# Group norm sums and factors in the free banks of the z panels, next group's transposes spread over the last two panels

## The chip, the cores and the metric

The kernel runs on one core of a Trainium2 chip (trn2). Its time is the device time of one execution in microseconds (us). Engines are named as in the profile: PE is the matrix engine (PEld its weight loads), DVE the vector engine, ACT the scalar engine, POOL the GpSimd engine, SP the engine that issues most loads.

## What is computed

The reference is a two-layer backbone over 512 latent and 256 context tokens of width 1024. Layer 0 mixes tokens with HGRN2, layer 1 with a bidirectional Mamba-2 scan; each ends with a SwiGLU network. The change lies in the Mamba-2 mixer:

```python
def prep(h):
    z, xbc, dt = jnp.split(h @ w_in, [SSM_D_INNER, SSM_D_INNER + SSM_CONV_DIM], axis=-1)
    xbc = jax.nn.silu(centred_depthwise_conv(xbc, conv_w, conv_b))
    xs, bm, cm = jnp.split(xbc, ...)
    ...
def readout(y_f, y_b, xs, z):
    y = (y_f + y_b + d_skip[:, None] * xs).reshape(bsz, m, SSM_D_INNER) * jax.nn.silu(z)
    y = rmsnorm(y.reshape(bsz, m, SSM_GROUPS, SSM_D_INNER // SSM_GROUPS),
                norm_w.reshape(SSM_GROUPS, -1)).reshape(bsz, m, SSM_D_INNER)
    return y @ w_out
```

There are 4 groups of 512 channels (8 heads of 64). A group's y is normalized over its own 512 channels: a sum of squares for each token, a factor 1/sqrt(mean + eps), and a product with both the factor and a weight.

## The kernel before, in words

Every float32 product is made of three float32r ones: an operand is split into a high part (`whi`, `hhi`, by ACT) and a low part (`wlo`, `hlo`, by DVE), and `product_block` (L309) issues high*high, high*low, low*high for one of the 8 slices k of the inner dimension. A **panel** is one 128-column slice of the weights: SP loads it to `raw`, ACT splits it at L292 (`whi`), DVE at L296 (`wlo`), PE multiplies it in 8 blocks of k. The weights of panel n+2 are split once panel n is finished. Panels take the two slots of the PSUM tensor G in turn; a slot has two banks of 512 columns. `Gq[:, b]` is bank b of G (0 and 1 are slot 0, 2 and 3 slot 1). The other four banks of PSUM are the tensor S; `PAIR[0]` is its banks 0 and 1, `PAIR[1]` its banks 2 and 3.

`ss_all` runs the mixer as a loop over groups in which **two groups overlap**. One call handles the ten panels j = 0 to 9 of group g (four x, b, c, four z) and, between their blocks, the scan and the norm of group q = g - 1. The first call has no q, three calls in a loop on the engines have both, the last has no g (there the blocks of the next product, `so_beside`, stand between). Panels 0 to 4 (x and b) cover all 768 tokens and need both banks of their slot; c and z (j = 5 to 9) cover 512 and use the first bank alone. Within a call (j, k) is a place on PE, after block k of panel j:

- j = 0 to 2: the chunk chain of q, 12 steps at every second k (`chain_tensor`, L1487 and L1491). Step n needs a weighted copy `wx` of `xtm`, made by DVE in `chain_values` (L1444). `chain_vector` makes `wx` of step n + 1, and at n = 0 also that of step 0.
- j = 3 to 6: the heads of q. (7, 3): transposes of their result `ytm` into S (L1605). DVE adds it to `yb` (semaphore `ya`), multiplies by z (`yz`), ACT squares (`ysq`), DVE adds the squares into `wx0` (L1568, `yr`).
- (8, 1): the sums over channels (L1610), to bank 0 of S. DVE makes the mean (L615), POOL the power (L620), and at (8, 4) PE spreads the factors over the partitions (L609), to bank 1 of S. DVE scales the four tiles of `yb` (L1578, `yn`), ACT makes their high parts (`ybhi`, L1424, `yh`), DVE their low parts (`yblo`, L1582, `yl`), and POOL stores both in memory (`y_park`, L1810).
- j = 9: six **turns** for the next chain, of group g: transposes of b into PAIR[0] (turn 0, L1625), the products of b and c into bank 2 of S (turn 1, L1628), four tiles of x (turns 2 to 5, L1633) into PAIR[0] and PAIR[1] in turn. ACT copies each out (`btm`, `cb`, `xtm`; L1428, L1431, L1434). Turn 0 waits until `yn` says that the factors in bank 1 have been read.

POOL's writes to `y_park` must have landed (`yout`) before ACT overwrites `yb` at j = 1 (L1409) and DVE writes `ytm` at chain step 4. All engines run their own queue in program order and wait for each other on semaphores only.

Of the kernel before, what the change touches and what calls it, by code (L numbers as in the profile page):

```python
# [199 lines left out]
def program(nc, x, c, ctx_x, c_ctx, ada_w, ada_b, norm_w, ffn_w_in, ffn_w_out, final_norm_w, hg_w_in, hg_lb,  # L200
            hg_norm_w, hg_w_out, ssm_w_in, ssm_conv_w, ssm_conv_b, ssm_dt_bias, ssm_a_log, ssm_d, ssm_norm_w,
            ssm_w_out, out):
    with ExitStack() as ctx:
# [1145 lines left out]
        def ss_scalar(act, dt, ss, g, q, prev):  # L1349
# [21 lines left out]
            for j in range(len(PANELS)):  # L1371
# [49 lines left out]
                if q is not None and j == 8:  # L1421
# [4 lines left out]
                if ss is not None and j == 9:  # L1426
                    act.wait_ge(s["ytr"], 6 * g + 1)
                    act.activation(m["btm"][:, :, :].rearrange("p b n -> p (b n)"), PAIR[0][:, 0:T], ACT.Copy)\  # L1428
                        .then_inc(s["stc"], 1)
                    act.wait_ge(s["ytr"], 6 * g + 2)  # L1430
                    act.activation(m["cb"][:, :], S[:, 2, :], ACT.Copy).then_inc(s["stc"], 1)  # L1431
                    for i_ in range(GT):
                        act.wait_ge(s["ytr"], 6 * g + 3 + i_)
                        act.activation(m["xtm"][:, :, i_ * P:(i_ + 1) * P],  # L1434
                                       PAIR[i_ % 2][:, 0:T].rearrange("p (b n) -> p b n", n=P), ACT.Copy)\
                            .then_inc(s["stc"], 1)
# [10 lines left out]
        def chain_vector(dve, q, n):  # L1447
            d, k, b = chain_at(n)
            st, own = m[f"st{d}"], states_of[d]
            if n == 0:  # L1450
                chain_values(dve, q, 0)
# [56 lines left out]
        def ss_vector(dve, dt, ss, g, q, prev):  # L1508
            for j in range(len(PANELS)):
# [60 lines left out]
                if q is not None and j == 8:  # L1570
                    dve.wait_ge(s["ysum"], q + 1)
                    mean_dve(dve, S[:, 0, 0:LBLK], GW)
# [3 lines left out]
                    for i_ in range(GT):  # L1576
                        yb = m["yb"][:, i_, :]
                        dve.scalar_tensor_tensor(yb, yb, m["colA"][:, bass.ds(q * GT + (COL_SN + i_), 1)],  # L1578
                                                 S[:, 1, :], ALU.mult, ALU.mult).then_inc(s["yn"], 1)
# [6 lines left out]
        TURNS = {0: 0, 1: 1, 2: 2, 3: 3, 5: 4, 7: 5}  # L1586

        def ss_between(pe, g, q, j, k):

            if q is not None:  # L1590
# [16 lines left out]
                if (j, k) == (8, 1):  # L1607
                    pe.wait_ge(s["yr"], GT * q + GT)
                    for b in range(LBLK):
                        ins = pe.matmul(S[:, 0, b:b + 1], block(m["wx0"][:, :], b), ones[:, :],  # L1610
                                        start=True, stop=True)
                    ins.then_inc(s["ysum"], 1)
                if (j, k) == (8, 4):
                    spread_pe(pe, q + RSTD_GROUPS, range(LBLK), S[:, 1, :])
            elif (j, k) == DT_TURN:
                dt_turn(pe)
            if g is not None and j == 9 and k in TURNS:
                n = TURNS[k]
# [522 lines left out]
```

## Time and profile before

| what | value |
|---|---|
| median of 3 runs | 2251.61 us (2251.16 to 2253.8) |
| profiled execution, its time | 2257.25 us |
| its span (first to last instruction) | 2254.3 us |
| PE busy | 2126.8 us, 94% of the span |
| DVE busy | 1091.2 us, 48% |
| ACT busy | 825.8 us, 37% |
| POOL busy | 50.4 us, 2% |
| granted PE clock, mean | 0.97 of full speed |

The median is 5.6 us below the profiled execution and 2.7 us below its span. The mixer's group loop lies at about 1338 to 1805 us of the span. A row of the timeline has the start, the length, engine, line, operation and, in brackets, how long the engine stood idle before it and on what. Matmuls overlap, so lengths on PE are longer than the distance from one start to the next. A float32 matmul is two instructions, so 4 of them are x8. In the "windows" rows PEclk is the granted clock as a share of 2.4 GHz: 1.00 is that level, 0.50 is 1.2 GHz, and values between are a mixture.

### The profile page before, as it was taken

How to read it: one execution, taken by the hardware profiler on the slowest of the kernel's cores; microseconds unless marked ns; L12 is line 12 of the kernel's file. 1: busy time of each engine (PE TensorE's matmuls, PEld its weight loads, DVE VectorE, ACT ScalarE, POOL GpSimd, SP SyncE). 2: the span in 40 equal slices, each digit the busy share in tenths (PEclk: the TensorE clock that was granted, in tenths of full speed). 3: DMA queues.
4: the chain of work that ended last, by engine and by line, in shares of the span. 5: the costliest groups of instructions: out<-in, count | busy, mean ns of one | idle time of the engine just before them, and what ended most of it. 6: DMA issues, size and time to landing. Idle time of an engine off the chain costs nothing.

```text
span 2254.3 us, 33844 instructions
## 1 busy us (share of the span) xinstructions
PE 2126.8 (94%) x13412; PEld 1892.8 (84%) x13412; DVE 1091.2 (48%) x1607; ACT 825.8 (37%) x1278; POOL 50.4 (2%) x79
## 2 busy tenths in 40 slices
PE   5899999999989999999999889999998898999998
PEld 3899999998889999999999867777775687888887
DVE  4755555557452222222234757767676545333334
ACT  2543334334232221122222454737382425532322
POOL 1000000000000000000000100000000000000000
PEclk8999999999989999999999989999999899999999
DMA  7322222213323332233321221221215232332332
GB/s 270 125 76 85 76 85 85 82 60 113 112 75 112 114 98 76 85 112 112 97 77 47 79 57 37 66 64 43 79 47 177 75 94 69 99 109 84 97 102 75
DMA packets 297512, 204.42 MB, mean 91 GB/s; under 512 B 5012, under 2 KB 289037, under 8 KB 295629
## 3 DMA queue, kind: packets, MB, share of 16 engines
q1 hardware_dynamic: 293965, 180.03, 26.4%
q0 software_dynamic: 3456, 23.09, 2.8%
q8 instruction: 68, 1.11, 0.2%
q14 instruction: 23, 0.19, 0.0%
HBM read 189.47 MB, written 13.63 MB: 90 GB/s over the span
## 4 chain that ended last, share of the span: by engine, by line
PE 78%; DVE 11%; ACT 7%; issue 3%; DMA 1%; SPq 0%; ACTq 0%; DVEq 0%; POOL 0%
PE G L309 65%; PE G L415 2%; PE S L1491 1%; ACT whi L292 1%; PE S L765 1%; DVE acc L1522 1%; ACT e L1367 1%; DVE hlo L646 1%; PE S L736 1%; PE S L1487 1%; DVE hn L638 1%; DVE wlo L296 1%; DVE cum L985 1%; PE S L1671 1%; PE G L421 1%
## 5 line engine op out<-in xcount | busy, mean ns | idle before, releaser
L309 PE MATMUL G<-hhi,whi 128*128 128x384 f32 (+2 forms) x2336 | 731.8, 371 | 31.2 <-DVE hlo L646 20.1
L309 PE MATMUL G<-hlo,whi 128*128 128x384 f32 (+2 forms) x2336 | 683.8, 351 | 0.0
L309 PE MATMUL G<-hhi,wlo 128*128 128x384 f32 (+2 forms) x2336 | 683.8, 351 | 0.0
L296 DVE TENSOR_TENSOR wlo<-raw,whi 128x1024 fp32r<-128x1024 f32 (+1 forms) x225 | 288.1, 1281 | 810.4 <-ACT whi L292 810.1
L292 ACT ACTIVATE whi<-raw 128x1024 fp32r<-128x1024 f32 (+1 forms) x225 | 248.7, 1106 | 958.0 <-PE G L309 487.5
L309 PEld LDWEIGHTS G<-hhi,whi 128*128 128x128 f32 x2336 | 425.2, 192 | 99.3 <-issue 36.3
L309 PEld LDWEIGHTS G<-hhi,wlo 128*128 128x128 f32 x2336 | 435.0, 191 | 20.7
L309 PEld LDWEIGHTS G<-hlo,whi 128*128 128x128 f32 x2336 | 435.8, 192 | 18.1
L309 PE MATMUL G<-mhi,whi 128*128 128x384 f32 (+2 forms) x550 | 165.6, 346 | 0.0
L309 PE MATMUL G<-mlo,whi 128*128 128x384 f32 (+2 forms) x550 | 165.2, 345 | 0.0
L309 PE MATMUL G<-mhi,wlo 128*128 128x384 f32 (+2 forms) x550 | 165.2, 345 | 0.0
L1522 DVE SCALAR_TENSOR_TENSOR acc<-xpad,colC,acc 128x770 f32<-128x770 f32 (+1 forms) x96 | 93.6, 975 | 35.2 <-ACT acc L1399 27.9
L309 PEld LDWEIGHTS G<-mhi,whi 128*128 128x128 f32 x550 | 101.2, 188 | 6.1
L309 PEld LDWEIGHTS G<-mlo,whi 128*128 128x128 f32 x550 | 101.3, 188 | 6.0
L309 PEld LDWEIGHTS G<-mhi,wlo 128*128 128x128 f32 x550 | 101.2, 188 | 6.0
L620 POOL TENSOR_TENSOR rstd<-stat,mhalf 128x6 f32<-128x6 f32 (+3 forms) x22 | 27.1, 1232 | 2097.7 <-DVE stat L615 2097.7
L1367 ACT ACTIVATE e<-S,shiftT 128x128 f32<-128x128 f32 x256 | 69.8, 394 | 9.2 <-PE S L1660 8.9
L1084 ACT ACTIVATE mhi<-mid 128x768 f32 (+3 forms) x44 | 32.5, 740 | 95.7 <-DVE mid L1104 95.7
L1135 DVE SCALAR_TENSOR_TENSOR x<-G,mods,x 128x384 f32 (+7 forms) x99 | 49.1, 533 | 20.0 <-PE G L309 18.5
L1491 PE MATMUL S<-wx,btm 128*128 128x512 f32 x80 | 45.0, 650 | 14.3 <-DVE wx L1444 14.3
L919 DVE SCALAR_TENSOR_TENSOR sin<-sin,gl,S 128x128 f32<-128x128 f32 x160 | 54.9, 348 | 6.7 <-PE S L736 1.6
L1108 DVE TENSOR_TENSOR mlo<-mid,mhi 128x768 f32 (+3 forms) x44 | 36.3, 825 | 44.2 <-ACT mhi L1084 44.2
(277 smaller groups left out, 2098.4 us busy)
## 6 DMA issues: line engine op xcount, KB each, us to landing
raw<-in_ffn_w_in_dram SPq DMA_DIRECT2D x88, 512.0 KB, 3.7
raw<-in_ffn_w_out_dram SPq DMA_DIRECT2D x32, 704.0 KB, 4.5
raw<-in_ssm_w_in_dram SPq DMA_DIRECT2D x41, 512.0 KB, 3.8
raw<-in_hg_w_in_dram SPq DMA_DIRECT2D x40, 512.0 KB, 3.9
adaw<-in_ada_w_dram SPq DMA_DIRECT2D x20, 1024.0 KB, 6.1
adaf<-in_ada_w_dram SPq DMA_DIRECT2D x20, 1024.0 KB, 5.0
ada<-in_ada_w_dram SPq DMA_DIRECT2D x4, 2048.0 KB, 13.2
raw<-in_ssm_w_out_dram SPq DMA_DIRECT2D x16, 512.0 KB, 3.9
```

Of the source, the lines that this page charges most:

```text
L292: act.activation(whi[pn.slot][:, 0:kt, :], raw[pn.slot][:, 0:kt, :], ACT.Copy).then_inc(s["hi"], 1)
L296: dve.tensor_tensor(wlo[pn.slot][:, 0:kt, :], raw[pn.slot][:, 0:kt, :], f32(whi[pn.slot][:, 0:kt, :]), ALU.subtract).then_inc(s["lo"], 1)
L309: ins = pe.matmul(G[:, tl.slot, g0:g0 + n], w[pn.slot][:, k, :], r[:, k_base + k, t0:t0 + n], start=(first and k == 0 and i == 0), stop=(l ...
L415: ins = pe.matmul(to[o:o + 2, :], m["csil"][:, k, :], w[:, k, :], start=(k < STRIPS), stop=(k >= KT - STRIPS))
L620: pool.tensor_tensor(m["rstd"][:, b0:b1], m["stat"][:, b0:b1], m["mhalf"][:, b0:b1], ALU.pow)\
L919: dve.scalar_tensor_tensor(to, sin[d][:, cc, :], gl[d][:, cc:cc + 1], new, ALU.mult, ALU.add).then_inc(own, 1)
L1084: act.activation(m["mhi"][:, bass.ds(i, 1), 0:nt].rearrange("p a t -> p (a t)"), m["mid0"][:, 0:nt], ACT.Copy).then_inc(s["mhi"], 1)
L1108: dve.tensor_tensor(m["mlo"][:, bass.ds(i, 1), 0:nt].rearrange("p a t -> p (a t)"), m["mid0"][:, 0:nt], f32(m["mhi"][:, bass.ds(i, 1), 0:n ...
L1135: ins = dve.scalar_tensor_tensor(xj, G[:, tl.slot, g0:g0 + n], gate, xj, ALU.mult, ALU.add)
L1367: ins = act.activation(block(m[f"e{d}{r}"][:, :], b), block(S[:, d, :], b), ACT.Exp, bias=m["shiftT"][:, b, bass.ds(q * HPG + (d * NH + hh ...
L1491: pe.matmul(S[:, d, :], m["btm"][:, b, :], m[f"wx{d}"][:, :], start=True, stop=True).then_inc(s["ds"], 1)
L1522: dve.scalar_tensor_tensor(m["acc"][:, 0:n], xpad[ci % 2][:, k:k + n], m["colC"][:, bass.ds(conv_tile(kind, i, g) + k * CONV_TILES, 1)], m ...
```

## The change

In a call with both groups the sums go to bank 1 of G and the factors to bank 3, the second banks of the slots, which z panels leave free. They stand at (8, 3) and (8, 6). The six turns stand at (8, 1), (8, 2), (8, 5), (8, 7), (9, 1), (9, 3). Turn 0 waits for `ya` (DVE has read the S banks) in place of `yn`; a new wait for `yn` stands at (9, 7), ahead of the next x panel, which needs bank 3. ACT copies turns 0 to 2 out at its step j = 8, turns 3 to 5 at j = 9, and only then makes `ybhi`. DVE makes the first `wx` of the next chain at j = 9 and the low parts `yblo` behind it; in the call before they stood at j = 8, ahead of the split of a panel. The first call keeps its six turns at their places, but its DVE too makes the first `wx` at j = 9. The last call keeps banks and places.

```diff
@@ ss_scalar (ACT)
-                if q is not None and j == 8:
+                if ss is not None:
+                    for n in ((0, 1, 2) if j == 8 else (3, 4, 5) if j == 9 else ()) if q is not None else range(6 * (j == 9)):
+                        turn_out(act, g, n)
+                if q is not None and j == (8 if ss is None else 9):
                     for i_ in range(GT):
                         act.wait_ge(s["yn"], q * GT + (i_ + 1))
                         act.activation(m["y3hi" if ss is None else "ybhi"][:, i_, :], m["yb"][:, i_, :], ACT.Copy)\
                             .then_inc(s["yh"], 1)
-                if ss is not None and j == 9:
-                    act.wait_ge(s["ytr"], 6 * g + 1)
-                    act.activation(m["btm"][:, :, :].rearrange("p b n -> p (b n)"), PAIR[0][:, 0:T], ACT.Copy)\
-                        .then_inc(s["stc"], 1)
...
+        def turn_out(act, g, n):
+            act.wait_ge(s["ytr"], 6 * g + n + 1)
+            if n == 0:
+                ins = act.activation(m["btm"][:, :, :].rearrange("p b n -> p (b n)"), PAIR[0][:, 0:T], ACT.Copy)
+            elif n == 1:
+                ins = act.activation(m["cb"][:, :], S[:, 2, :], ACT.Copy)
+            else:
+                ins = act.activation(m["xtm"][:, :, (n - 2) * P:(n - 1) * P],
+                                     PAIR[n % 2][:, 0:T].rearrange("p (b n) -> p b n", n=P), ACT.Copy)
+            ins.then_inc(s["stc"], 1)
@@ chain_vector (DVE)
-            if n == 0:
-                chain_values(dve, q, 0)
@@ ss_vector (DVE)
                 if q is not None and j == 8:
                     dve.wait_ge(s["ysum"], q + 1)
-                    mean_dve(dve, S[:, 0, 0:LBLK], GW)
+                    mean_dve(dve, group_sums(ss)[:, 0:LBLK], GW)
...
-                                                 S[:, 1, :], ALU.mult, ALU.mult).then_inc(s["yn"], 1)
+                                                 group_factors(ss), ALU.mult, ALU.mult).then_inc(s["yn"], 1)
+                if ss is not None and j == 9:
+                    chain_values(dve, g, 0)
+                if q is not None and j == (8 if ss is None else 9):
                     for i_ in range(GT):
                         dve.wait_ge(s["yh"], q * GT + (i_ + 1))
...
-        TURNS = {0: 0, 1: 1, 2: 2, 3: 3, 5: 4, 7: 5}
-
-        def ss_between(pe, g, q, j, k):
+        def group_sums(ss):
+            return S[:, 0, :] if ss is None else Gq[:, 1, :]
+        def group_factors(ss):
+            return S[:, 1, :] if ss is None else Gq[:, 3, :]
+        TURNS_FIRST = {(9, 0): 0, (9, 1): 1, (9, 2): 2, (9, 3): 3, (9, 5): 4, (9, 7): 5}
+        TURNS = {(8, 1): 0, (8, 2): 1, (8, 5): 2, (8, 7): 3, (9, 1): 4, (9, 3): 5}
+        SUMS_BESIDE, SPREAD_BESIDE = (8, 3), (8, 6)
+        def ss_between(pe, ss, g, q, j, k):
...
-                if (j, k) == (8, 1):
+                if (j, k) == ((8, 1) if ss is None else SUMS_BESIDE):
...
-                if (j, k) == (8, 4):
-                    spread_pe(pe, q + RSTD_GROUPS, range(LBLK), S[:, 1, :])
+                if (j, k) == ((8, 4) if ss is None else SPREAD_BESIDE):
+                    spread_pe(pe, q + RSTD_GROUPS, range(LBLK), group_factors(ss))
+                if ss is not None and (j, k) == (9, KT - 1):
+                    pe.wait_ge(s["yn"], q * GT + GT)
...
-            if g is not None and j == 9 and k in TURNS:
-                n = TURNS[k]
+            turns = TURNS_FIRST if q is None else TURNS
+            if g is not None and (j, k) in turns:
+                n = turns[j, k]
                 if n == 0:
                     pe.wait_ge(s["conv"], 6 * g + 6)
-                    pe.wait_ge(s["dtT"], 1)
-                    if q is not None:
-                        pe.wait_ge(s["yn"], q * GT + GT)
+                    if q is None:
+                        pe.wait_ge(s["dtT"], 1)
+                    else:
+                        pe.wait_ge(s["ya"], q * GT + GT)
```

On PE, panel 8 of the loop, before: the sums (L1610, waiting for `yr`) are the first thing between the blocks.

```order
L309 MATMUL G<-hlo,whi_71 128x512
L309 MATMUL G<-hhi,wlo_72 128x512
L1608 ISA
L1610 MATMUL S<-ones,wx_168 128x1 [waits s_yr]
L1610 MATMUL S<-ones,wx_168 128x1 x3
L309 MATMUL G<-hhi,whi_71 128x512
L309 MATMUL G<-hlo,whi_71 128x512
L309 MATMUL G<-hhi,wlo_72 128x512
```

The same place after; L1642 and L1645 are turns 0 and 1, L1623 the sums.

```order
L1640 ISA [waits s_conv]
L1642 MATMUL S<-ident,bfm 128x128 [waits s_ya]
L1642 MATMUL S<-ident,bfm 128x128 x5
L309 MATMUL G<-hhi,whi_71 128x512
L309 MATMUL G<-hlo,whi_71 128x512
L309 MATMUL G<-hhi,wlo_72 128x512
L1645 MATMUL S<-cfm,bfm 128x128 x4
L309 MATMUL G<-hhi,whi_71 128x512
L309 MATMUL G<-hlo,whi_71 128x512
L309 MATMUL G<-hhi,wlo_72 128x512
L1623 MATMUL G<-ones,wx_168 128x1 [waits s_yr]
L1623 MATMUL G<-ones,wx_168 128x1 x3
```

Two turns and two blocks have moved ahead of the sums. On DVE, from the end of a call over the loop's edge, before:

```order
L1582 TENSOR_TENSOR yblo<-yb,ybhi 128x512 [waits s_yh] x4
L295 REGISTER_ALU
L296 TENSOR_TENSOR wlo_72<-raw_68,whi_71 128x1024 [waits s_hi]
L1677 REGISTER_ALU
L1677 COMPARE_AND_BRANCH
L296 TENSOR_TENSOR wlo_70<-raw_67,whi_69 128x1024 [waits s_hi]
L1533 CAST sel<-ident 64x8 x4
L1444 TENSOR_TENSOR wx_168<-xtm,wT 128x512 [waits s_stc]
L1444 TENSOR_TENSOR wx_169<-xtm,wT 128x512
L1477 COPY st_170<-S 128x512 [waits s_ds]
```

And after:

```order
L296 TENSOR_TENSOR wlo_72<-raw_68,whi_71 128x1024 [waits s_hi]
L1447 ISA [waits s_stc]
L1447 TENSOR_TENSOR wx_168<-xtm,wT 128x512
L1586 TENSOR_TENSOR yblo<-yb,ybhi 128x512 [waits s_yh] x4
L1694 REGISTER_ALU
L1694 COMPARE_AND_BRANCH
L296 TENSOR_TENSOR wlo_70<-raw_67,whi_69 128x1024 [waits s_hi]
L1534 CAST sel<-ident 64x8 x4
L1447 TENSOR_TENSOR wx_169<-xtm,wT 128x512
L1478 COPY st_170<-S 128x512 [waits s_ds]
```

The first `wx` has moved ahead of the edge; `wx1`, of step 1, stays behind the split and the four casts. On ACT, steps j = 8 and 9, before:

```order
L292 ACTIVATE whi_69<-raw_67 128x1024 [waits s_pan]
L1381 ISA
L1381 ACTIVATE z<-G 128x512
L1424 ACTIVATE ybhi<-yb 128x512 [waits s_yn] x4
L291 REGISTER_ALU [waits s_raw1]
L292 ACTIVATE whi_71<-raw_68 128x1024 [waits s_pan]
L1381 ISA
L1381 ACTIVATE z<-G 128x512
L1428 ACTIVATE btm<-S 128x768 [waits s_ytr]
L1431 ACTIVATE cb<-S 128x512 [waits s_ytr]
L1434 ACTIVATE xtm<-S 128x6x128 [waits s_ytr] x3
```

And after:

```order
L1433 ACTIVATE btm<-S 128x768 [waits s_ytr]
L1435 ACTIVATE cb<-S 128x512 [waits s_ytr]
L1437 ACTIVATE xtm<-S 128x6x128 [waits s_ytr]
L291 REGISTER_ALU [waits s_raw1]
L292 ACTIVATE whi_71<-raw_68 128x1024 [waits s_pan]
L1381 ISA
L1381 ACTIVATE z<-G 128x512
L1437 ACTIVATE xtm<-S 128x6x128 [waits s_ytr] x2
L1431 REGISTER_ALU
L1437 ACTIVATE xtm<-S 128x6x128 [waits s_ytr]
L1427 ACTIVATE ybhi<-yb 128x512 [waits s_yn] x4
```

The high parts of y have moved behind all copies, to the end of the call.

## Rows read from the trace of the kernel before

**Rows 1.** The page: the chain that ended last, by engine.

```profile
PE 78%; DVE 11%; ACT 7%; issue 3%; DMA 1%; SPq 0%; ACTq 0%; DVEq 0%; POOL 0%
```

**Rows 2.** Waits of PE, 1330:1830: who waited for whom, total, times, longest.

```profile
PE S L1491 <- DVE wx L1444: 14.3, 5, 4.2
PE S L1610 <- DVE wx L1568: 11.1, 4, 4.2
```

**Rows 3.** Timeline of PE, first loop call, panel 7 to the next panel 0.

```profile
1441.17 1.10 PE L1671 MATMUL S<-xtm,e 128*128 128x64 f32 x8 [1.42 <-DVE e L1500]
...
1449.18 0.39 PE L309 MATMUL G<-hhi,wlo 128*128 128x512 f32 x1
1451.98 1.05 PE L1610 MATMUL S<-ones,wx 128*128 128x1 f32 x8 [2.42 <-DVE wx L1568]
...
1458.23 0.40 PE L309 MATMUL G<-hhi,whi 128*128 128x512 f32 x1
...
1458.92 0.39 PE L309 MATMUL G<-hhi,whi 128*128 128x512 f32 x1
...
1460.71 0.84 PE L1625 MATMUL S<-ident,bfm 128*128 128x128 f32 x6 [0.27 <-DVE yb L1578]
...
1469.70 0.59 PE L309 MATMUL G<-hhi,whi 128*128 128x384 f32 x2
...
1474.17 2.00 PE L1491 MATMUL S<-wx,btm 128*128 128x512 f32 x2 [3.17 <-DVE wx L1444]
...
1478.86 1.02 PE L1491 MATMUL S<-wx,btm 128*128 128x512 f32 x2
...
1481.80 1.02 PE L1491 MATMUL S<-wx,btm 128*128 128x512 f32 x2
```

**Rows 4.** Timeline of PE at the other three joints, in order of time.

```profile
1347.68 0.59 PE L309 MATMUL G<-hhi,whi 128*128 128x384 f32 x2
...
1352.16 2.08 PE L1491 MATMUL S<-wx,btm 128*128 128x512 f32 x2 [3.17 <-DVE wx L1444]
...
1357.87 1.20 PE L1491 MATMUL S<-wx,btm 128*128 128x512 f32 x2
...
1574.33 1.05 PE L1610 MATMUL S<-ones,wx 128*128 128x1 f32 x8 [2.39 <-DVE wx L1568]
...
1591.89 0.59 PE L309 MATMUL G<-hhi,whi 128*128 128x384 f32 x2
...
1600.99 1.02 PE L1491 MATMUL S<-wx,btm 128*128 128x512 f32 x2
...
1696.21 1.87 PE L1610 MATMUL S<-ones,wx 128*128 128x1 f32 x8 [2.09 <-DVE wx L1568]
...
1714.93 0.82 PE L1633 MATMUL S<-ident,xfm 128*128 128x128 f32 x6
1719.98 4.62 PE L1491 MATMUL S<-wx,btm 128*128 128x512 f32 x6 [4.23 <-DVE wx L1444]
```

**Rows 5.** Timeline of DVE, first loop call: norm, and start of the chain.

```profile
1457.84 2.72 DVE L1578 SCALAR_TENSOR_TENSOR yb<-yb,colA,S 128x512 f32<-128x512 f32 x4 [4.61 <-PE S L609]
...
1471.77 1.23 DVE L296 TENSOR_TENSOR wlo<-raw,whi 128x1024 fp32r<-128x1024 f32 x1 [7.66 <-ACT whi L292]
...
1473.43 1.29 DVE L1444 TENSOR_TENSOR wx<-xtm,wT 128x512 f32<-128x512 f32 x2
```

**Rows 6.** Timeline of ACT, same call.

```profile
1458.63 2.61 ACT L1424 ACTIVATE ybhi<-yb 128x512 fp32r<-128x512 f32 x4 [6.27 <-DVE yb L1578]
...
1469.98 0.81 ACT L1434 ACTIVATE xtm<-S 128x768 f32<-128x768 f32 x1 [1.24 <-PE S L1633]
1470.69 1.05 ACT L292 ACTIVATE whi<-raw 128x1024 fp32r<-128x1024 f32 x1
```

**Rows 7.** Windows, PE alone: stretch, length, PE busy (instructions), PEclk, DMA share, GB/s.

```profile
1352.00:1358.00 6.00, 5.84 (x15) 0.50 0.33 89
...
1453.50:1457.50 4.00, 4.00 (x17) 0.57 0.46 131
```

**Rows 8.** DMA issues: size each, median us from issue to landing.

```profile
y_park_lo<-yblo POOLq DMA_DIRECT2D x3, 1024.0 KB, 6.4
```

More of the change, by code:

```diff
@@ L1425, in ss_scalar @@
                             .then_inc(s["yh"], 1)
-                if ss is not None and j == 9:
-                    act.wait_ge(s["ytr"], 6 * g + 1)
-                    act.activation(m["btm"][:, :, :].rearrange("p b n -> p (b n)"), PAIR[0][:, 0:T], ACT.Copy)\
-                        .then_inc(s["stc"], 1)
[L1430 to L1436, printed above, removed]
+        def turn_out(act, g, n):
[8 more added lines that the diff above has]
+            ins.then_inc(s["stc"], 1)
         def chain_values(dve, q, n):
@@ L1606, in ss_between @@
                         ins.then_inc(s["ytt"], 1)
-                if (j, k) == (8, 1):
+                if (j, k) == ((8, 1) if ss is None else SUMS_BESIDE):
                     pe.wait_ge(s["yr"], GT * q + GT)
                     for b in range(LBLK):
-                        ins = pe.matmul(S[:, 0, b:b + 1], block(m["wx0"][:, :], b), ones[:, :],
+                        ins = pe.matmul(group_sums(ss)[:, b:b + 1], block(m["wx0"][:, :], b), ones[:, :],
                                         start=True, stop=True)
                     ins.then_inc(s["ysum"], 1)
-                if (j, k) == (8, 4):
-                    spread_pe(pe, q + RSTD_GROUPS, range(LBLK), S[:, 1, :])
+                if (j, k) == ((8, 4) if ss is None else SPREAD_BESIDE):
+                    spread_pe(pe, q + RSTD_GROUPS, range(LBLK), group_factors(ss))
+                if ss is not None and (j, k) == (9, KT - 1):
+                    pe.wait_ge(s["yn"], q * GT + GT)
             elif (j, k) == DT_TURN:
                 dt_turn(pe)
-            if g is not None and j == 9 and k in TURNS:
-                n = TURNS[k]
+            turns = TURNS_FIRST if q is None else TURNS
+            if g is not None and (j, k) in turns:
+                n = turns[j, k]
                 if n == 0:
                     pe.wait_ge(s["conv"], 6 * g + 6)
-                    pe.wait_ge(s["dtT"], 1)
-                    if q is not None:
-                        pe.wait_ge(s["yn"], q * GT + GT)
+                    if q is None:
+                        pe.wait_ge(s["dtT"], 1)
+                    else:
+                        pe.wait_ge(s["ya"], q * GT + GT)
                     for b in range(NBLK):
@@ L1641, in ss_tensor @@
                     product(pe, ss + j, ss + j, m["hhi"], m["hlo"], KT, LAT if kind in "zc" else SEGS,
-                            between=lambda k: ss_between(pe, g, q, j, k))
+                            between=lambda k: ss_between(pe, ss, g, q, j, k))
                 else:
                     for k in range(KT):
-                        ss_between(pe, None, q, j, k)
+                        ss_between(pe, None, None, q, j, k)
                         for _ in range(SO_BESIDE.get((j, k), 0)):
```

## The prediction

> **What bounds the kernel now.** I read the chain that ended last first: 78% of it is PE [rows 1]. So what counts is where PE stands still, and the view for that is the list of waits. In the mixer's loop two waits lead it: the first chain step waits 14.3 us in 5 places for `wx`, and the sums wait 11.1 us in 4 places for the squares [rows 2]. One of the four, in the last call, isn't touched by the change. The timeline then shows what stands around each wait. In panel 8 PE reaches (8, 1) at about 1449.4, finds `wx0` not summed and starts the sums at 1451.98 [rows 3]. Behind it come two blocks, the factors, and in panel 9 all six turns. At the next panel 0 PE does one block and stands for 3.17 us. The timelines of ACT and DVE say why: the last copy of x starts at 1469.98, `whi` follows it at once, `wlo` starts at 1471.77, then come four casts, and the first `wx` starts at 1473.43 [rows 5, 6]. This `wx` has had its data since 1470.8; it stands late only because it is behind a split in DVE's program.
>
> The windows show the second price. After the sums' wait the granted clock is 0.57 of full over 1453.5 to 1457.5, and after the first joint's wait it is 0.50 for 6 us [rows 7]; 0.50 is the 1.2 GHz level. After the 1.42 us wait at 1441.17 [rows 3] the blocks run on at full pace. So each long wait costs itself and a slow stretch, and I take both from distances between starts.
>
> **Part 1: from (8, 1) to the next panel 0.** The work is the same before and after: 14 blocks, six turns, sums, factors. Its length without waits at the full clock: from turn 0 at 1460.71 to panel 0 at 1469.70 are 7 blocks and six turns, 9.0 us. The other 7 blocks take 0.69 each (1458.23 to 1458.92, three matmuls), 4.8. Sums 1.05 by their row; the factors are 8 matmuls too, I take 1.05 again. Sum 15.9 us [rows 3]. Before, the stretch begins where PE went idle (start of the sums less the idle time less 0.15 for the end of the last matmul) and takes 1449.4 to 1469.7 = 20.3; 1571.8 to 1591.9 = 20.1; 1694.0 to 1715.5 = 21.5 (the last turn at 1714.93 plus 0.6) [rows 3, 4]. If all waits go, the gain is 4.4 + 4.2 + 5.6 = **14.2 us**. Of it 7.3 are the waits themselves, the rest is slow clock and 0.3 to 0.4 before turn 0.
>
> Do they go? Sums: PE now does turn 0 (0.6), turn 1 (0.8) and two blocks (1.5) before them and comes at 1452.3, with the squares' sum ready at 1451.9. Margin 0.4 us; if I am off by that, the cost is as much for each call. Turn 0 needs `ya`, which DVE has done some 3 us before. Factors: three blocks and turn 2 lie between them and the sums, 2.8 us; before it was three blocks. They come at 1456.1 and DVE scales from about 1457.3 to 1460.3 (2.72 for four, rows 5), while the new wait at (9, 7) is reached at 1465.3. Cover 5 us, cost nothing; the wait holds back only panel 0. Turns: each needs the copy of the turn two before it. ACT's copies take 0.8 each; the tightest is turn 5 at 1462.3, behind the copy of turn 3, which on ACT stands behind `whi` and z of panel 8 and ends about 1460.6. Cost nothing, cover 1.7 us. DVE's split of a panel at j = 9 is needed only at 1465.3 and comes no later.
>
> **Part 2: the joint, panel 0 to the second chain step.** Without a wait: one block 1.15 (1469.70 to where the idle 3.17 begins), then step 0 and two blocks, 2.94 (1478.86 to 1481.80), together 4.1 us [rows 3]. Before it took 10.2, 9.2 and 9.1 us (1347.68 to 1357.87; 1469.70 to 1478.86; 1591.89 to 1600.99) [rows 3, 4]. After, counted from panel 0's start E: in the first call the turns stay, the copy of the last ends at E + 1.1 and `wx` of 0.65 at E + 1.8, while PE is there at E + 1.15. A wait of 0.7 us stays. In the loop the last turn is at (9, 3), 3.4 us before E, its copy ends at E - 1.8 and `wx0` is ready at E - 1.1. That wait goes whole. Next is `wx1`: ACT makes the four `ybhi` (2.6, rows 6) from E - 1.9 to E + 0.7, `whi` to E + 1.75, DVE `wlo` to E + 3.0, casts 0.5, `wx1` to **E + 4.1**; PE wants it at E + 4.1. So it just meets, and I charge 0.1. Gains 5.4 + 5.0 + 4.9 = **15.3 us**, if the slow stretch goes with the wait; a remaining 0.7 is well below the 1.42 that left no trace.
>
> **Part 3: the last call's start** has no panel beside it. PE waits 4.23 us, then DVE is the busier [rows 4]. After, DVE has one `wx` less in the row (0.65) and needn't wait for step 0's matmul (about 1.5). Bounds 0.65 and the whole 4.4; I take **2.2**, the sum of the two.
>
> **Part 4: what moves later.** `yblo` ends at E + 1.5 where it ended 7 us before E, so the store of it is issued at about E + 1.8. It lands 6.4 us later [rows 8], E + 8.2. ACT's next write of `yb` and DVE's chain step 4 wait for it; that step comes at E + 13 in the loop and E + 11 in the last call. Cover 3 to 5 us, cost nothing. In the last call POOL's reloads of y go out 2 us later and behind two stores of 1 MB; the first product that reads them comes 17 us after E. Cost nothing to 2 us. Sum: 14.2 + 15.3 + 2.2 = 31.7; I take off 0.7 for hand-overs that came out as just meeting. **31 us**: the execution of span 2254.3 would have 2223, and the median 2251.6 becomes **2220.6**.
>
> **Rivals.** (a) The wait moves one chain step on: `wx1` comes at the lag it has now, E + 5.0, so 0.95 us for each loop joint, and with that the slow stretches at the joints stay (2.8 + 1.7 + 1.7). For it: the margin is zero, and ACT has 2.6 us of `ybhi` ahead of `whi`. Against it: a wait of 1.42 us left the clock alone. 8 us of the gain go: 2229. (b) The slow stretch behind the sums isn't due to the wait. Its half level begins 1.7 us after PE has resumed, not in the wait, and PE was full before and after. Then 6.5 us of part 1 stay: 2227. The Trainium skill ("TensorE: Matmul & The Clock Gate", section on HAM oscillation) ties the slow clock to idle gaps above a length; if 2.4 us is too short, its rule gives this rival, and the trace, with a slow stretch behind all three such waits, speaks rather against it. (c) The change gains nothing: the waits go, but panels 0 to 2 are held by the taps and the chain on DVE. PE's back-to-back steps of 2.94 speak against it. 2251. (d) **Slower**: the stores of y hold the next group. Place: DVE's chain step 4 at (1, 0), with PE's steps behind it; price: each us that a store lands after E + 11 to 13, in three calls, at once on the path. It decides from a landing time of 9 to 11 us in place of 6.4 and passes the 31 us gained only from about 20 us each; nothing in the rows comes near. 2260.
>
> **How the numbers follow.** Forecast 0.68, (a) 0.12, (b) 0.10, (c) 0.03, (d) 0.02, more gain than summed (last call's 4.4 whole, further slow stretches gone) 0.05. The range goes from 2214 (34.6 by the upper bounds, and 3 us of clock) to 2234 ((a) and (b) in good part together). Faster by over 0.2% (4.5 us, about what a measurement of this kernel can tell): 0.95; within 0.2%: 0.03; slower: 0.02.
>
> **What would show it.** In the profile after, the waits of PE should have no row of the sums in the three loop calls, the one for `wx` should be one of about 0.7 us in the first call and the last call's; windows over panels 8, 9 and 0 should show PEclk 1.00; panel 8's (8, 1) to panel 0 should take 16 us, panel 0 to step 1 4.1 to 4.5. The clock is the weakest step: if half-level stretches stand where no wait is, I am wrong by up to 13 us. Next comes `wx1`.

## The result, and the profile after

| | before | after |
|---|---|---|
| median, us (range, executions) | 2251.97 (2251.16 to 2253.8, 4) | 2224.68 (2224.3 to 2229.35, 4) |
| profiled execution, us | 2257.25 | 2224.3 |
| its span, us | 2254.3 | 2222.4 |
| its mean granted clock | 0.970 | 0.977 |

The changed kernel takes 0.9882 of the time before (95% interval 0.9866 to 0.9898): 27 us less by the medians, with 30 to 23 us inside the interval. The forecast was 31 us less, at 2220.6, in a range of 2214 to 2234. It held. A second comparison of the same two kernels (below) gave 0.9856 (0.9841 to 0.9871), 32 us less by the ratio and 31 by the medians.

The first thing to see is PE's list of waits over the same stretch as [rows 2], 1330 to 1830 (waiting engine and line, who was waited for, total us, times, longest):

```profile
PE S L1675 <- ACT e L1367: 7.0, 7, 2.4
...
PE S L1623 <- DVE wx L1569: 4.2, 1, 4.2
PE S L1492 <- DVE wx L1447: 3.5, 2, 2.9
```

The sums (L1610 before, L1623 now) waited 11.1 us in four places and now wait 4.2 in one, the last call's, which the change leaves alone. The first chain step (L1491 before, L1492 now) waited 14.3 us in five places and now 3.5 in two: 0.58 in the first call and 2.90 in the last. That is 17.7 us of waiting gone. The waits on `e`, inside the heads, lead the list now (7.0 us, 6.9 before).

PE's timeline of the first loop call, to be laid beside [rows 3] (start, us, engine, line, operation, out<-in, count, idle time before it):

```profile
1444.69 0.82 PE L1642 MATMUL S<-ident,bfm 128*128 128x128 f32 x6
...
1447.64 0.95 PE L1623 MATMUL G<-ones,wx 128*128 128x1 f32 x8
...
1460.36 0.51 PE L309 MATMUL G<-hhi,whi 128*128 128x384 f32 x2
...
1461.42 1.02 PE L1492 MATMUL S<-wx,btm 128*128 128x512 f32 x2
...
1464.40 1.02 PE L1492 MATMUL S<-wx,btm 128*128 128x512 f32 x2
```

Turn 0, turn 1 and two blocks stand where PE used to wait, the sums follow without idle time, and the next panel 0 starts 15.67 us after turn 0. Its second chain step comes 4.04 us after panel 0. Both have been at full pace all the way, as windows of PE alone say (stretch, length, PE busy and instructions, PEclk, DMA share, GB/s); [rows 7] had 0.50 and 0.57 at these places, that is at or near the lower of TensorE's two levels, 1.2 in place of 2.4 GHz:

```profile
1346.40:1351.40 5.00, 4.42 (x24) 1.00 0.04 7
1444.00:1460.00 16.00, 16.00 (x99) 1.00 0.25 66
1460.00:1465.00 5.00, 5.00 (x26) 1.00 0.62 226
```

So the gain can be split in two. Over 1330 to 1800, the time at the lower level fell from 54.5 us to 27.3 (each window's length times twice what its clock lacks to 1.00). PE is nearly always busy there, so this gives back about half of it, 13.6 us. With the 17.7 us of waits that makes 31.3, beside 31.9 measured between the two spans. (Outside this stretch the time at the lower level hardly changed, 81.1 us before and 79.1 after.)

The start of the last call, which [rows 4] show at 1719.98 with a wait of 4.23 us, and the first call's joint:

```profile
1348.31 1.13 PE L1492 MATMUL S<-wx,btm 128*128 128x512 f32 x2 [0.58 <-DVE wx L1447]
...
1351.36 1.02 PE L1492 MATMUL S<-wx,btm 128*128 128x512 f32 x2
...
1688.28 4.64 PE L1492 MATMUL S<-wx,btm 128*128 128x512 f32 x6 [2.90 <-DVE wx L1447]
```

### The profile page after: what moved, and what is told of

Its sections match the earlier page's. It is cut to its first block, busy times and chain, and to the rows that moved or that the text cites. A ratio compares the mean times of both kernels' runs of the same rounds, so it can differ in the third digit from the quotient of the medians.

```text
span 2222.4 us, 33823 instructions
## 1 busy us (share of the span) xinstructions
PE 2111.2 (95%) x13397; PEld 1882.9 (85%) x13412; DVE 1091.4 (49%) x1607; ACT 824.9 (37%) x1278; POOL 49.1 (2%) x79
## 4 chain that ended last, share of the span: by engine, by line
PE 79%; DVE 10%; ACT 6%; issue 3%; DMA 1%; SPq 0%; ACTq 0%; DVEq 0%; POOL 0%
PE G L309 66%; PE G L415 2%; PE S L765 1%; PE S L1492 1%; DVE acc L1523 1%; ACT whi L292 1%; ACT e L1367 1%; DVE hlo L646 1%; PE S L736 1%; PE S L1488 1%; DVE wlo L296 1%; DVE hn L638 1%; PE S L1688 1%; DVE cum L985 1%; PE G L421 1%
## 5 line engine op out<-in xcount | busy, mean ns | idle before, releaser
L309 PE MATMUL G<-hhi,whi 128*128 128x384 f32 (+2 forms) x2336 | 726.8, 369 | 31.7 <-DVE hlo L646 20.5
L1523 DVE SCALAR_TENSOR_TENSOR acc<-xpad,colC,acc 128x770 f32<-128x770 f32 (+1 forms) x96 | 93.7, 976 | 36.2 <-ACT acc L1399 28.3
L573 ACT ACTIVATE hhi<-hn,mods 128x128 fp32r<-128x128 f32 (+2 forms) x64 | 30.2, 503 | 51.6 <-DVE hn L638 51.6
```

Of the source, the lines that this page charges most:

```text
L309: ins = pe.matmul(G[:, tl.slot, g0:g0 + n], w[pn.slot][:, k, :], r[:, k_base + k, t0:t0 + n], start=(first and k == 0 and i == 0), stop=(l ...
L573: ins = act.activation(m["hhi"][:, v % KT, t0:t0 + n], hn_of(N, v)[:, t0:t0 + n], ACT.Identity, bias=mod(l, 3 * i, v % KT, g))
L1523: dve.scalar_tensor_tensor(m["acc"][:, 0:n], xpad[ci % 2][:, k:k + n], m["colC"][:, bass.ds(conv_tile(kind, i, g) + k * CONV_TILES, 1)], m ...
```

## Experiments

Each ratio is to the kernel before, run on the same chip beside it, with its 95% interval. "Slow stretch" is short for one in which the windows show PEclk near 0.50. The kernel before was measured three times more beside them, at 2252.95, 2253.15 and 2252.3 us in the median.

### The change again

The same kernel a second time, as the measure for those beside it.

> The changed kernel itself, once more, beside its variants. Expected: 2224.7 us as measured, ratio to before 0.988. If the 1.24 us that it was ahead before the first changed instruction was chance, the ratio stays where the median had it and not where the profiled spans had it (0.986).

Measured: 2221.76 us (2219.72 to 2225.39, 4 executions), 0.9856 (0.9841 to 0.9871). The two intervals for the same change, around 0.9882 and 0.9856, only just meet. The ratio came out where the two profiled spans had it (0.986). The lead of 1.2 us ahead of the first changed instruction didn't recur: panel 0 of the second call starts at 1347.59 here, at 1346.44 in the first profile and at 1347.68 before. From this panel 0 to the first block that multiplies the last group's own y (`y3hi`, in the last call) the two profiles of the changed kernel take 423.9 and 423.8 us. This stretch is called the changed part from here on; the kernel before takes 455.4 us for it (1347.68 to 1803.09).

### Each half of the change alone

`sums_only` keeps the free banks and the early turns, but puts the first `wx` back where it stood:

```diff
         def chain_vector(dve, q, n):
+            if n == 0:
+                chain_values(dve, q, 0)
...
-                if ss is not None and j == 9:
-                    chain_values(dve, g, 0)
```

> After, but the first wx is made as before, at the start of the next call behind the split and the casts. Part 1 alone. My theory: the stretch from (8, 1) to panel 0 takes 15.7 us as in after (gain 14.2 to 14.9 in all), the joints wait about 3.0 us for wx0 and have the half clock behind it (8.8 us in the loop, 10.2 in the first call): 2252 - 15 = 2237. Rival (b), slow stretches that aren't due to the wait: 2243.

`wx_only` is the kernel before with nothing but the first `wx` moved ahead of the next panel's split on DVE:

```diff
-            if n == 0:
-                chain_values(dve, q, 0)
...
                         dve.tensor_tensor(m["yblo"][:, i_, :], m["yb"][:, i_, :],
...
+                if ss is not None and j == 9:
+                    chain_values(dve, g, 0)
```

> Before, and DVE makes the first wx at j = 9. Part 2 alone. My theory: the last turn stays at (9, 7), so wx0 comes 1.8 us after panel 0's start, where PE is at 1.15: 0.7 us of wait stays at each joint and the clock stays full. Gains 5.4 + 4.4 + 4.3, and 2 in the last call: 2236. The waits for the sums stay at 2.2 to 2.6 us with their slow stretches. Rival: the slow stretch at the joint stays though the wait is short: 2242.

Measured: `sums_only` 2237.39 us (2233.72 to 2240.76, 5), 0.9932 (0.9918 to 0.9945), so 15 us gained by the ratio and 16 by the medians, as expected; `wx_only` 2241.82 us (2241.43 to 2246.3, 5), 0.9954 (0.9941 to 0.9968), so 10 or 11 us. Together 26 or 27, beside 27 and 32 for the whole: within what can be told here the halves add up, and neither needs the other.

`wx_only` came 6 us above its expected time, and its trace doesn't show these 6 us. Its joints did what was expected (waits of 0.57 to 0.70 us, 4.9 to 5.1 us from panel 0 to step 1), and its changed part takes 440.1 us, 15.4 less than before, where 16.1 were expected. That of `sums_only` takes 434.6, or 20.8 less. So each half gains 4 to 5 us more between the profiles than between the medians, and the two together (36.2) more than the whole change (31.5). The 455.4 us before come from a single profiled execution, of 2257.25 us, 5 above the median; that it was slow in the loop would explain all of this, but it isn't shown.

The slow stretches behind the sums stayed in two of three calls. PE's timeline of `wx_only`, the sums (L1610) and their factors (L609) in the first and the third loop call:

```profile
1446.87 1.05 PE L1610 MATMUL S<-ones,wx 128*128 128x1 f32 x8 [2.38 <-DVE wx L1566]
...
1449.93 1.05 PE L609 MATMUL S<-ident,rstd 128*128 128x128 f32 x8
...
1681.89 1.86 PE L1610 MATMUL S<-ones,wx 128*128 128x1 f32 x8 [2.06 <-DVE wx L1566]
...
1687.60 1.54 PE L609 MATMUL S<-ident,rstd 128*128 128x128 f32 x8
```

Between sums and factors lie the same blocks each time, but from start to start it was 3.06 us here, 5.71 there, and 3.98 in the second call, behind a wait of 2.39. The three waits are nearly alike, and what follows them isn't. `sums_only` shows the same at its joints, where the first `wx` is waited for again:

```profile
1350.64 2.08 PE L1494 MATMUL S<-wx,btm 128*128 128x512 f32 x2 [3.17 <-DVE wx L1447]
...
1356.36 1.02 PE L1494 MATMUL S<-wx,btm 128*128 128x512 f32 x2
...
1467.13 1.12 PE L1494 MATMUL S<-wx,btm 128*128 128x512 f32 x2 [2.50 <-DVE wx L1447]
...
1470.18 1.02 PE L1494 MATMUL S<-wx,btm 128*128 128x512 f32 x2
```

A wait of 3.17 us was followed by a step at half pace (5.72), one of 2.50 by a step at full pace (3.05).

### Does the wait make the slow stretch?

This is what rival (b) denied for the sums. The next two kernels leave the waits' causes alone and keep PE at work in them, with bf16 multiplications into a free bank, whose products nobody reads. If the idle time makes the slow stretch, it goes though the sums come no earlier. `fill_sums`, on the kernel before:

```diff
                 if (j, k) == (8, 1):
+                    if g is not None:
+                        for _ in range(10):
+                            pe.matmul(Gq[:, 1, :], m["identb"][:, :], m["neg0"][:, :], start=True, stop=True)
                     pe.wait_ge(s["yr"], GT * q + GT)
```

> Before, with 10 extra bf16 matmuls of 128x512 (about 2.2 us) on PE at (8, 1) ahead of the wait for the squares, to a bank that nobody reads. PE is busy in the wait, and the wait's end is where it was. My theory: the slow stretch is due to the wait, so it goes: 1.5 + 1.8 + 3.1 = 6.4 us less, 2245.6. Rival (b): the slow stretch has another cause and stays: 2252.

`fill_joint` has 13 of the same at (0, 0), ahead of the first chain step:

```diff
             if q is not None:
+                if g is not None and (j, k) == (0, 0):
+                        for _ in range(13):
+                            pe.matmul(Gq[:, 1, :], m["identb"][:, :], m["neg0"][:, :], start=True, stop=True)
                 if j < 3 and k % 2 == 0:
```

> Before, with 13 such matmuls (2.8 us) at (0, 0) ahead of the wait for the first wx in the loop's three calls. My theory: the slow stretches behind the joints go, 2.8 + 1.7 + 1.7 = 6.2 us less, 2245.8. Rival (b): 2252.

Measured: `fill_sums` 2248.66 us (2244.08 to 2251.36, 11), 0.9975 (0.9965 to 0.9984); `fill_joint` 2246.03 us (2245.67 to 2250.06, 6), 0.9972 (0.9959 to 0.9984). Both are faster than the kernel before, by 4.5 and 7.1 us of the medians, though they only add work. `fill_joint` is at its expected time, `fill_sums` 3 us above it. PE's timeline of `fill_sums` in the first loop call (the fillers, the sums, the factors):

```profile
1452.48 2.33 PE L1610 MATMUL G<-neg,identb 128*128 128x512 bf16 x10
...
1455.05 1.05 PE L1613 MATMUL S<-ones,wx 128*128 128x1 f32 x8 [0.24 <-DVE wx L1568]
...
1458.13 1.05 PE L609 MATMUL S<-ident,rstd 128*128 128x128 f32 x8
```

The sums come as late as ever, but from them to the factors it is now 3.08, 3.05 and 3.05 us in the three calls, where the kernel before took 4.13, 3.65 and 5.71: 4.3 us gained by these distances, where 6.4 were expected. `fill_joint`, first loop call:

```profile
1470.09 2.98 PE L1593 MATMUL G<-neg,identb 128*128 128x512 bf16 x13
...
1473.42 1.12 PE L1491 MATMUL S<-wx,btm 128*128 128x512 f32 x2 [0.35 <-DVE wx L1444]
...
1476.47 1.02 PE L1491 MATMUL S<-wx,btm 128*128 128x512 f32 x2
```

Step 0 to step 1 takes 3.05 us here, and 3.04 and 3.05 at the other two joints (4.69, 5.71 and 4.62 before, [rows 3, 4]). At its sums, where nothing was filled, the slow stretches stayed, in three calls of three. So the slow stretches need the idle time: rival (b) has fallen. That the fillers only shifted them is unlikely: 16 of the 21 unfilled waits of this kind were followed by one (table at the end), and none of the six filled ones.

### What gives the first half: the turns in the wait, or the later sums?

`sums_first` is the changed kernel with the sums at (8, 1) and the factors at (8, 4) again, still in the free banks, and turns 0 and 1 behind the sums:

```diff
-        TURNS = {(8, 1): 0, (8, 2): 1, (8, 5): 2, (8, 7): 3, (9, 1): 4, (9, 3): 5}
-        SUMS_BESIDE, SPREAD_BESIDE = (8, 3), (8, 6)
+        TURNS = {(8, 2): 0, (8, 3): 1, (8, 5): 2, (8, 7): 3, (9, 1): 4, (9, 3): 5}
+        SUMS_BESIDE, SPREAD_BESIDE = (8, 1), (8, 4)
```

> After, but the sums stay at (8, 1) and the factors at (8, 4) (in their new banks), with turns 0 and 1 at (8, 2) and (8, 3). It keeps the free banks and undoes the filling of the wait. My theory: PE waits 2.4 us for the squares again in each of the three calls, the joints stay at 4.1 us: 7.2 us of waits and 0 to 6 us of slow clock come back, 2229 to 2236. If what counts is only that the turns end early, the same as after: 2222 to 2225.

Measured: 2235.79 us (2234.14 to 2236.86, 5), 0.9923 (0.991 to 0.9937), 11 to 14 us more than the two medians of the changed kernel. The wait is back, alone (waits of PE, 1330 to 1830; the others are as in the changed kernel):

```profile
PE G L1623 <- DVE wx L1569: 7.3, 3, 2.4
```

7.3 us of waits, and a slow stretch in two of three calls. The free bank alone doesn't fill the wait; it allows the turns to stand ahead of the sums, and that is worth these 11 to 14 us (9.6 between the changed parts of the profiles). The kernel is still 6 us faster than `wx_only`, which has neither the free banks nor the earlier turns: its waits for `wx` are 3.5 us in place of 5.1, and the rest isn't taken apart by any run.

### How close is the second `wx`?

The prediction had the second `wx` just meeting PE, and made rival (a) of it. `late_whi` delays ACT's split of the next panel by two copies of 0.63 us that nobody reads:

```diff
                             .then_inc(s["yh"], 1)
+                    if ss is not None:
+                        for i_ in (0, 1):
+                            act.activation(m[f"sc{i_}"][:, :], m["cb"][:, :], ACT.Copy)
```

> After, with two extra copies of 0.63 us on ACT behind ybhi, so that the split of the next panel comes 1.27 us later. My theory: the joint just meets, so each of the two loop joints waits 1.3 us for wx1 and the last call starts 1.3 us later: 3.9 us slower, 2228.6; the clock stays full, since waits up to 1.42 us left it alone. Rival (a)'s clock part: a wait of 1.3 us brings the half clock back, 1.7 us more at each joint: 2232. If the joint had slack: 2224.7.

Measured: 2225.14 us (2223.22 to 2227.08, 4), 0.9877 (0.9862 to 0.9892), 3.4 us more than the changed kernel beside it. PE's timeline at the first loop joint:

```profile
1460.23 1.02 PE L1495 MATMUL S<-wx,btm 128*128 128x512 f32 x2
...
1463.93 1.13 PE L1495 MATMUL S<-wx,btm 128*128 128x512 f32 x2 [0.56 <-DVE wx L1450]
```

A delay of 1.26 us moved the step by 0.72 (3.70 from step 0 in place of 2.98), so about 0.5 us of slack stood in the way. The other loop joint moved by 0.71 and the start of the last call by 0.84, 2.3 us in all; the expectation without slack was 3.9. The next step follows at 1466.98, 3.05 us on and at full pace: the wait of 0.56 us cost itself and no clock.

`wx1_early` goes the other way: the second `wx` is made right behind the first, ahead of the split.

```diff
-            if n + 1 < 2 * NBLK:
+            if 1 < n + 1 < 2 * NBLK:
                 chain_values(dve, q, n + 1)
...
                 if ss is not None and j == 9:
                     chain_values(dve, g, 0)
+                    chain_values(dve, g, 1)
```

> After, and DVE makes the wx of step 1 too at j = 9, ahead of yblo. My theory: the loop joints have nothing left (step 1 started 2.98 us after step 0 where 2.94 is the pace), so they give 0.1 in all; in the last call PE's wait of 2.9 us for wx1 goes, but DVE, not PE, sets the pace there and has one wx (0.65 us) less behind the split, so 0.6 us: 2224. Rival: the wait of 2.9 us was on the path and goes whole: 2221.8.

> wx1_early once more, beside its variants. By its trace it is 0.9 us shorter than after in the last call and equal elsewhere; the 4 us between the medians were fewer slow stretches between the heads. If these fall by chance, it now lies at 2218 to 2223; if its places bring them about, at 2217.5 again.

Measured: 2217.53 us (2216.68 to 2219.36, 5), 0.9841 (0.9827 to 0.9854), and again 2218.93 us (2216.49 to 2229.46, 5), 0.9859 (0.9838 to 0.988). The first is below everything that was expected for it (2221.8 to 2224). The second lies between its two cases and decides nothing; one of its executions, 2229.46, is as slow as the slowest of the changed kernel. At the loop joints nothing changed (2.98 us from step 0 to 1), since the slack was there. In the last call the start shortened by 0.93 us in the first profile, and by 0.2 in the second, where a slow stretch lies in it; the wait went one step on:

```profile
1687.87 2.30 PE L1492 MATMUL S<-wx,btm 128*128 128x512 f32 x4 [3.46 <-DVE wx L1447]
```

The medians lie 3 to 7 us below those of the changed kernel, and the changed part takes 417.5 and 417.9 us in place of 423.9 and 423.8. Only 0.9 us of that is shown by the waits. The rest goes with fewer slow stretches (13.7 and 20.5 us at the lower level over 1330 to 1800 in its two profiles, 27.3 and 27.2 in the two of the changed kernel). Two that are gone in both profiles stood in the heads of the first and the third loop call, behind PE's wait for `e` at (7, 1), which was 1.5 to 1.75 us and is 1.4 now. Why they are fewer stays open: the next kernel waits as briefly there and has all three.

### The first joint's last 0.6 us

`wx1_first_turns` is `wx1_early` with the first call's last two turns one and two blocks earlier, so that the first `wx` is ready in time:

```diff
-        TURNS_FIRST = {(9, 0): 0, (9, 1): 1, (9, 2): 2, (9, 3): 3, (9, 5): 4, (9, 7): 5}
+        TURNS_FIRST = {(9, 0): 0, (9, 1): 1, (9, 2): 2, (9, 3): 3, (9, 4): 4, (9, 5): 5}
```

> As wx1_early, and in the first call turns 4 and 5 stand at (9, 4) and (9, 5) in place of (9, 5) and (9, 7), so the last copy ends 1.4 us earlier. My theory: the first joint's wait of 0.58 us goes: 0.6 us less than wx1_early, 2223.5. Rival: turn 4 then waits for the copy of turn 2 (0.8 us each on ACT), and nothing is gained.

Measured: 2223.71 us (2222.44 to 2226.21, 4), 0.9866 (0.9851 to 0.9881). The wait of 0.57 us is gone, and the kernel is 6 us slower than `wx1_early` beside it. That it meets the expected 2223.5 is luck: 0.6 us less than `wx1_early` was expected. The same windows of both, between the heads of the three loop calls, first `wx1_first_turns`:

```profile
1438.00:1444.00 6.00, 6.00 (x32) 0.72 0.32 87
1550.00:1556.00 6.00, 5.36 (x27) 0.72 0.32 87
1662.00:1668.00 6.00, 4.65 (x22) 0.75 0.29 85
```

and `wx1_early`:

```profile
1438.00:1444.00 6.00, 6.00 (x36) 1.00 0.32 90
1550.00:1556.00 6.00, 6.00 (x38) 1.00 0.32 87
1662.00:1668.00 6.00, 6.00 (x36) 1.00 0.20 61
```

Behind the short waits in the heads (1.4 us, the same in both) one profile has three slow stretches and the other none. Each makes the way to the sums 1.6 us longer, 4.9 in all; the first joint gives back 0.9. That is 3.9 of the 6.2 us between the two spans. The other 2.3 stand ahead of the first call's panel 0 (1350.74 against 1348.39), and already ahead of the turns that were moved. No execution of the one is as fast as the slowest of the other beside it. Why the earlier turns call the stretches up isn't shown: no run here varied the shift by itself.

### Filling what is left

`fill_last` is `wx1_early` with fillers in the last call: 18 ahead of the sums, 11 ahead of the factors. `fill_all` has besides 4 and 6 of them at (6, 4) and (7, 1) of the loop calls, to fill the waits for `e`. Their products aren't read.

```diff
+                if ss is None and (j, k) in ((8, 1), (8, 3)):
+                    pe.wait_ge(s["ya"], GT * q + GT)
+                    for _ in range(18 if k == 1 else 11):
+                        pe.matmul(S[:, 3, :], m["identb"][:, :], m["neg0"][:, :], start=True, stop=True)
```

```diff
+                if ss is not None and (j, k) in ((6, 4), (7, 1)):
+                    for _ in range(4 if j == 6 else 6):
+                        pe.matmul(Gq[:, 1, :], m["identb"][:, :], m["neg0"][:, :], start=True, stop=True)
```

> wx1_early, and in the last call extra bf16 matmuls that nobody reads in the two waits of PE: 18 (3.9 us) in the 4.2 us wait for the squares at (8, 1), 11 (2.4 us) in the 2.5 us wait for a split at (8, 3). In after a half-level stretch of 10.2 us stands there. My theory: it goes, 10.2 us at half level cost up to 5, so 3 to 5 us less than wx1_early. If slow clock came from something else than standing still: no change.

> fill_last, and in the loop's calls 4 such matmuls (0.9 us) at (6, 4) in a wait of 1.1 us and 6 (1.3 us) at (7, 1) in a wait of 1.4 us, between the heads. The slow stretches that stand there in some calls (0 to 3 of 3 by run, up to 1.7 us each) should go: 0 to 4 us less than fill_last, and less spread among the runs. If the extra matmuls don't fit the waits, up to 1 us more for each call.

Measured: `fill_last` 2217.75 us (2215.81 to 2219.97, 5), 0.9843 (0.983 to 0.9857); `fill_all` 2217.43 us (2216.62 to 2217.93, 5), 0.9842 (0.9829 to 0.9856). The same window over the last norm, first `wx1_early`, then `fill_last`:

```profile
1748.00:1768.00 20.00, 13.65 (x53) 0.74 0.18 53
```

```profile
1748.00:1768.00 20.00, 19.58 (x94) 1.00 0.18 53
```

From the sums to the first `y3hi` block it was 14.0 us and is 10.8. Three microseconds are gained at this place, and they can't be seen in the time: the medians of `wx1_early` are 2217.53 and 2218.93. In the profiled execution of `fill_last` other slow stretches, behind the edit, ate them: from the first `y3hi` block to the end it takes 453.9 us, with 20.8 us at the lower level behind 1800, where both profiles of `wx1_early` take 451.2, with 10.7 and 10.8. `fill_all` has the narrowest spread of all, 1.3 us, and no better median. Its fillers at (7, 1) take the wait of 1.4 us away; those at (6, 4) stand 5 us behind the wait of 1.1 us that they were meant for, which stays in all three calls. The best kernels of this study are `wx1_early` and its two successors, at about 2217.5 us, some 5 us below the changed kernel.

## Why the prediction was right, and what of it was off

**Part 1, (8, 1) to panel 0.** Forecast 15.9 us in each call, measured 15.67 in all three (1444.69 to 1460.36, 1555.87 to 1571.54, 1668.69 to 1684.36). From 20.3, 20.1 and 21.5 that gains 4.6, 4.4 and 5.8, together 14.9; forecast 14.2. Its inner steps held too. PE comes to the sums 2.95 us behind turn 0 (forecast 2.9). The margin there, 0.4 us, is real and thin. DVE's timeline has the squares summed at 1447.18, and PE reads them at 1447.64:

```profile
1445.69 1.49 DVE L1569 TENSOR_TENSOR wx<-wx,sc 128x512 f32<-128x512 f32 x2 [0.76 <-ACT sc L1420]
```

**Part 2, the joint.** Forecast 4.1 us, measured 4.04 and 4.04 in the loop and 4.92 in the first call, whose wait of 0.7 was forecast and is 0.58. Gains 5.3, 5.1, 5.1, together 15.5; forecast 15.3. That `wx1` just meets was right in kind. Here are DVE and ACT in the first loop call, to lay beside [rows 5, 6]:

```profile
1458.77 0.69 DVE L1447 TENSOR_TENSOR wx<-xtm,wT 128x512 f32<-128x512 f32 x1 [2.44 <-ACT xtm L1437]
1459.38 2.49 DVE L1586 TENSOR_TENSOR yblo<-yb,ybhi 128x512 fp32r<-128x512 f32 x4
1461.79 1.22 DVE L296 TENSOR_TENSOR wlo<-raw,whi 128x1024 fp32r<-128x1024 f32 x1
...
1463.44 0.69 DVE L1447 TENSOR_TENSOR wx<-xtm,wT 128x512 f32<-128x512 f32 x1
```

```profile
1458.51 2.18 ACT L1427 ACTIVATE ybhi<-yb 128x512 fp32r<-128x512 f32 x4
1460.59 1.05 ACT L292 ACTIVATE whi<-raw 128x1024 fp32r<-128x1024 f32 x1
```

The forecast took 2.6 us for the four `ybhi`; they took 2.18, since nothing of theirs was waited for. So `whi` was ready at E + 1.3 and not E + 1.75, and `wlo` started behind DVE's own `yblo` and not behind ACT. `wx1` ended at E + 3.8 in place of E + 4.1. PE starts step 1 another 0.3 us later. With the 0.2 us that `whi` is ready ahead of DVE, this is the half microsecond of slack that `late_whi` found. The 0.7 us that the sum took off for hand-overs weren't needed. Rival (a), a wait that moves one step on, had the right mechanism (in the last call it did), and about 0.5 us of slack kept it away from the loop's joints.

One argument against (a) was misread. "A wait of 1.42 us left the clock alone" comes from the first loop call. The same wait of the kernel before in the other two calls, 1.39 and 1.41 us, was followed by a stretch of 3.4 us at the lower level each time. In the second call:

```profile
1561.96 1.10 PE L1671 MATMUL S<-xtm,e 128*128 128x64 f32 x8 [1.39 <-DVE e L1500]
```

The windows are shown below. It did no harm: the one wait that stayed at the joints, 0.6 us, is shorter still.

**Part 3, the last call's start.** From where the call starts on PE (1715.50 before, behind the last turn; 1684.36 after) to its first block of the next product 16.94 us became 14.78: 2.2, as forecast. The two bounds that were added were not measured apart.

**Part 4, the stores.** They go out at E + 1.8, as forecast (1462.17), and take 6.9 us in place of 6.4. The rows of DMA issues after (size, median us from issue to landing; before it was 6.4 for the store, [rows 8], and 11.5 for the reload):

```profile
y_park_lo<-yblo POOLq DMA_DIRECT2D x3, 1024.0 KB, 6.9
...
ylo<-y_park_lo POOLq DMA_DIRECT2D x3, 1024.0 KB, 16.8
```

The reload takes 5 us more, and in the last call others wait for the late store. From the list of all engines' waits over 1330 to 1830:

```profile
ACT yb L1409 <- DMA y_park_lo<-yblo: 7.0, 1, 7.0
POOL yhi L1819 <- DMA y_park_lo<-yblo: 4.6, 1, 4.6
```

ACT stands for 7.0 us, and PE has no row for it: who waited for the reload was PE's weight load alone, 0.3 us. The cover held, and rival (d) fell.

**The sum.** The named parts come to 14.9 + 15.5 + 2.2 = 32.6 us where 31.7 were forecast, and the span fell by 31.9 where 31 were.

**Rivals.** (b) is refuted by `fill_sums` and `fill_joint`; (c) by the result. By the median, 2224.68, the outcome lies between the forecast and (a) or (b), 2227 to 2229. The trace and not the time has decided against these: both waits and both slow stretches are gone.

**What was off** is the last step, from one execution to the median. The forecast took 31 us of the span off the median. But the profiled execution of the kernel before lay 5 us above its own median, and that of the changed kernel at its median. The medians then moved by 27 us where the spans moved by 32. Of the difference 1.2 us can be placed: the first call's panel 0 started at 1346.44 in place of 1347.68 before any changed instruction of PE. The rest probably stood in the loop, as the halves suggest; there is no second profile of the kernel before to show it. The two comparisons, 27 and 32 us, put the change's worth at 29 or 30.

**The weakest step**, named as such, was that slow stretches might stand where no wait was removed. They did, behind the wait for `e` at (7, 1), and that they cancelled is luck. The windows of PE alone, after, then before:

```profile
1435.00:1440.00 5.00, 5.00 (x25) 0.66 0.38 105
...
1562.00:1567.00 5.00, 5.00 (x34) 1.00 0.22 65
```

```profile
1435.00:1440.00 5.00, 4.75 (x25) 1.00 0.35 99
1562.00:1567.00 5.00, 5.00 (x24) 0.66 0.40 105
```

In the first loop call the wait (1.73 us after, at 1434.84; 1.42 before) is newly followed by a slow stretch, and from the start of the matmuls behind it to (8, 1) it takes 9.9 us in place of 8.2. In the second call (1.53 us after, at 1547.64; 1.39 before) the stretch is gone, and it takes 8.2 in place of 9.8. In the third both kernels have one.

## What to carry to other kernels

If PE waits for a result that another engine makes, look for work of PE's own that stands behind the wait only for want of a free bank, and put it ahead; a narrow result fits a bank that the tile beside it leaves unused. Look just as closely at the program order of the engine that is waited for: one instruction of 0.65 us had its data and stood behind a split nobody needed yet, and moving it gave 10 us by itself. Price a wait of PE by distances between starts on both sides of it, since the slow clock behind it can cost nearly as much again (here 13.6 us on top of 17.7), and where the wait can't go, throwaway multiplications in a free bank give that part back.

## What the runs showed of the chip

**Which waits bring the clock down.** The sums of the loop calls, the three joints and the waits for `e` in the heads of the loop calls, over all profiles of this study (the last call, where other work stands around the waits, isn't counted):

| PE's idle time, us | followed by a slow stretch |
|---|---|
| 3.17 | 6 of 7 |
| 2.0 to 2.5 | 10 of 14 |
| 1.4 to 1.8 (in the heads) | 17 of 39 |
| 1.1 (in the heads) | none of 42 |
| up to 0.7 | none |

The forecast's picture, in which a wait either does this or doesn't, was too simple: the same wait at the same place does it in one kernel and not in the next. In the heads all three of one kernel were followed by a slow stretch and none of its neighbour's, at the same 1.4 us. Filled with other PE work it happened in none of nine: six sums and joints, and the three at (7, 1) of `fill_all`. The Trainium skill ("TensorE: Matmul & The Clock Gate", section on HAM oscillation) ties the slow clock to idle gaps above a length, and all the waits in this table are shorter than that length. The measurements decide: 2.0 to 2.5 us were followed by the lower level in ten cases of fourteen.

**How far a time of this kernel can be told.** The part up to 1330 us is the same in all the kernels of this study, and spent between 64.8 and 75.2 us at the lower level in their profiled executions, whatever the edit. Each microsecond of that can cost up to half a microsecond of time. The mean granted clock goes with the time of the single executions too: of the eight of the changed kernel, the slowest (2229.35 us) had 0.974 and the two fastest (2219.72 and 2219.79) 0.978. That is probably why the same change was measured at 27 and at 32 us, and why a gain of 3 us that the windows show plainly, as in `fill_last`, doesn't show in medians of five executions.
